# Compressing the decode requests' pages inside the first query tiles of the prompt attention

## The reference

```python
def cmp_sub(kv, w_cmp):
    B, T = kv.shape[:2]
    kb = kv.reshape(B, T // D_CMP, D_CMP, 2, KV_HEADS, N_HEAD_DIM)
    first = jnp.einsum('bnpchd,cpde->bnche', kb, w_cmp[:, :D_CMP])
    second = jnp.einsum('bnpchd,cpde->bnche', kb, w_cmp[:, D_CMP:])
    return first, second

def compress_blocks(first, second, w_cmp, pe_cmp):
    bias = jnp.einsum('cpd,cpde->ce', pe_cmp, w_cmp)
    return first[:, :-1] + second[:, 1:] + bias[None, None, :, None, :]
```

## Time and profile before

| | |
|---|---|
| Median of 3 runs | 1217.35 us (1217.02 to 1221.65) |
| Profiled execution, its own time | 1223.5 us |
| Its span | 1221.7 us, 14579 instructions |
| PE busy | 1127.9 us (92%) |
| DVE / ACT / POOL busy | 478.2 / 325.7 / 71.8 us |
| Mean granted clock of TensorE | 0.953 of full |
| Chain that ended last | PE 84%, DVE 9%, ACT 3%, issue 2%, DMA 1% |

### The profile page before, as it was taken

How to read it: one execution, slowest core, us unless ns; L and a number is a source line. 1 busy time by engine, 2 the same in 40 slices (tenths; PEclk the granted TensorE clock), 3 DMA queues, 4 the chain that set the end, 5 groups by cost and what they waited for, 6 DMA issues and landing times.

```text
span 1221.7 us, 14579 instructions
## 1 busy us (share of the span) xinstructions
PE 1127.9 (92%) x5447; PEld 664.1 (54%) x5447; DVE 478.2 (39%) x1025; ACT 325.7 (27%) x791; POOL 71.8 (6%) x181
## 2 busy tenths in 40 slices
PE   5999999999999999999789999999967869679997
PEld 4566644444455656966554566665555628244442
DVE  6453430001112221323377776776545443421121
ACT  4421100000011111100256666676641102001110
POOL 1000000000000001110111000010050002000000
PEclk9999999999999999999789999999977869879999
DMA  9202010203100303110210000000042543722221
GB/s 321 120 1 69 1 69 0 71 3 68 44 28 1 80 13 88 41 57 1 83 57 1 1 2 1 1 2 1 1 135 86 139 130 116 236 69 69 69 69 43
DMA packets 70222, 73.00 MB, mean 60 GB/s; under 512 B 28411, under 2 KB 54695, under 8 KB 70087
## 3 DMA queue, kind: packets, MB, share of 16 engines
q1 hardware_dynamic: 70150, 72.06, 19.4%
HBM read 62.14 MB, written 14.07 MB: 62 GB/s over the span
## 4 chain that ended last, share of the span: by engine, by line
PE 84%; DVE 9%; ACT 3%; issue 2%; DMA 1%; SPq 0%; POOL 0%; ACTq 0%; DVEq 0%; POOLq 0%
PE PS L1893 25%; PE PS L1886 12%; PE PS L2235 10%; PE PS L2001 7%; PE PS L2020 5%; PE PS L2033 5%; PE PS L1937 3%; PE PS L2173 2%; PE PS L2169 1%; PE PS L1923 1%; DVE VV L1665 1%; PE PS L2007 1%; PE PS L2126 1%; ACT XT L1113 1%; PE PS L1891 1%
## 5 line engine op out<-in xcount | busy, mean ns | idle before, releaser
L1893 PE MATMUL PS<-WR,XT 128*128 128x512 f32 (+1 forms) x768 | 306.9, 557 | 0.0
L1893 PEld LDWEIGHTS PS<-WR,XT 128*128 128x128 f32 x768 | 144.0, 190 | 147.7 <-issue 144.6
L1886 PE MATMUL PS<-XT,WR 128*128 128x352 f32 x576 | 172.2, 460 | 1.1 <-ACT QN L998 1.1
L1886 PEld LDWEIGHTS PS<-XT,WR 128*128 128x128 f32 x576 | 108.8, 190 | 61.2 <-ACT QN L998 1.6
L1493 DVE TENSOR_REDUCE XT<-PS 128x1 f32<-128x640 f32 (+7 forms) x128 | 84.5, 701 | 37.7 <-PE PS L2007 37.7
L2001 PE MATMUL PS<-KTR,XT 64*128 64x512 f32 (+3 forms) x384 | 92.8, 502 | 5.8 <-ACT XT L1113 5.4
L1113 ACT ACTIVATE XT<-PS,XT 128x640 f32<-128x640 f32 (+7 forms) x96 | 66.7, 701 | 10.4 <-DVE XT L1493 10.4
L2001 PEld LDWEIGHTS PS<-KTR,XT 64*128 64x128 f32 x384 | 45.7, 192 | 36.9 <-issue 16.8
L2020 PE MATMUL PS<-cst,XT 128*128 128x128 f32 x396 | 61.9, 281 | 0.8 <-ACT MT L1126 0.8
L2235 PE MATMUL PS<-WR,QT 128*128 128x512 f32 x128 | 57.6, 593 | 0.6 <-DVE XT L1733 0.6
L2235 PE MATMUL PS<-WR,KT 128*128 128x512 f32 x128 | 57.5, 592 | 0.0
(11 more groups left out here) (445 smaller groups left out, 1358.7 us busy)
## 6 DMA issues: line engine op xcount, KB each, us to landing
WR<-in_w_in SPq DMA_DIRECT2D x24, 512.0 KB, 6.3
WR<-in_cache_kv_cmp SPq DMA_DIRECT2D x48, 128.0 KB, 2.5
WR<-in_w_in SPq DMA_DIRECT2D x32, 128.0 KB, 3.1
KVN<-in_cache_kv_sel SPq DMA_DIRECT2D x32, 128.0 KB, 2.1
GM<-in_cache_kv_sel SPq DMA_DIRECT2D x32, 128.0 KB, 2.0
QN<-in_cache_kv_win SPq DMA_DIRECT2D x8, 512.0 KB, 5.6
XT<-in_x_prompt SPq DMA_DIRECT2D x8, 512.0 KB, 4.1
out_y_prompt<-XT SPq DMA_DIRECT2D x8, 512.0 KB, 2.9
```

The lines of the kernel that those rows point to most:

```text
L1886: ins = mm(b[:, 0:THIRD], w[:, k, r // 3 * P:(r // 3 + 1) * P], xt[:, k, r % 3 * THIRD:(r % 3 + 1) * THIRD], **f)
L1893: ins = mm(b[:, 0:width], xt[:, k, r * P:(r + 1) * P], w[:, k, :], **f)
```

## The change

The eight requests are compressed in pairs 0 to 25 of the prompt attention. In pair p < 24 TensorE turns chunk p mod 3 of request p // 3, in every third pair the fourth chunk as well; from pair 2 on one half of the products, the other half, and the turn of the values follow in rotation. Products use PSUM bank 3, chunks bank 1, which short tiles leave free. ScalarE's copies and VectorE's sums take the matching places in their lists, GpSimd sorts in tiles 0 to 3. SyncE loads all eight requests' compressed pages in a row (three buffers instead of four), then the output weights and the first half's window rows, all during the attention. The results lie in `kc_all` and `vc_all` until the decode step reads them. The turned weights are stored in another order of dimensions. The decode step has no compression left.

```diff
...
+        def chunk_of(p):
+            return (p // 3, p % 3) if p < 3 * SB else None
+        def event_of(p):
+            return (("cmp", (p - 2) // 3, (p - 2) % 3) if (p - 2) % 3 < 2 else ("turn", (p - 2) // 3, 0)) \
+                if 2 <= p < 2 + 3 * SB else None
...
-            for b in range(4):
+            for b in range(SB):
                 load_cmp(b)
...
+            sp.wait_ge(cm_sorted, SB + 1)
+            for c in range(KC):
...
+            sp.wait_ge(qr_turned, NT)
+            load_windows(0)
...
             sp.wait_ge(num_done, MH)
             load_pages(0, 0)
-            for g in range(2):
-                sp.wait_ge(cmp_done, 2 * (4 * g + 4 + 1))
-                load_windows(g)
-                if g == 0:
-                    for b in range(4, SB):
-                        load_cmp(b)
-                    sp.wait_ge(g_pe, GPE(0, "sel"))
-                    load_pages(1, 1)
-                    load_pages(1, 0)
...
-            sp.wait_ge(cm_sorted, SB + 1)
-            for c in range(KC):
...
+            sp.wait_ge(g_pe, GPE(0, "sel"))
+            load_pages(1, 1)
+            load_pages(1, 0)
+            sp.wait_ge(g_pe, GPE(0, "win"))
+            load_windows(1)
...
+            def sort_sample(b):
+                pool.wait_ge(cm_s_in[b % 3], (b // 3 + 1) * NPG * 16)
+                if b >= 2:
+                    pool.wait_ge(cx_turned, 4 * (b - 1) + 4)
+                for a in range(4):
+                    ins = nc.gpsimd.tensor_copy(sorted_s[b % 2][a].rearrange("p (c r d) -> p c r d", c=4, r=2),
+                                                cms[b % 3][:, a, :].rearrange("p (r c d) -> p c r d", c=4, r=2))
+                ins.then_inc(cm_sorted, 1)
             pool.wait_ge(proj_done, ALL)
+            nc.gpsimd.memset(kc_all, 0.0).then_inc(blocks_zeroed, 1)
...
                 rotate(x, trig[:, i, :], NH, rq).then_inc(q_rot, 1)
+                if i in (2, 3):
+                    sort_sample(4 if i == 2 else 7)
...
                 nc.gpsimd.tensor_tensor(p8, p8, sum8.unsqueeze(2).broadcast_to([P, NH, NCMP]), ALU.mult).then_inc(pc_scaled, 1)
...
-            pool.wait_ge(qr_turned, NT)
-            sort_sample(0)
+                if i == 0:
+                    pool.wait_ge(vc_ready, 1)
+                for b in ((0, 1), (2, 3), (5, 6))[i] if i < 3 else ():
+                    sort_sample(b)
...
-            sort_sample(1)
-            pool.wait_ge(cm_sorted, 3)
...
+            def take_pairs(b, ch):
+                act.wait_ge(cx_turned, 4 * (b + 1) + ch + 1)
+                if b and ch % 2 == 0:
+                    act.wait_ge(cmp_done, 2 * b + ch // 2 + 1)
+                nc.scalar.activation(cx_s[:, ch // 2, ch % 2, :, :], bank(1).rearrange("p (n s) -> p s n", s=8), ACT.Copy)\
+                    .then_inc(cx_ready, 1)
...
                 if p + 1 < NT * PAIRS:
                     for h in range(KVH):
                         exps(p + 1, h)
+                chunk = chunk_of(p)
+                if chunk:
+                    take_pairs(*chunk)
                 take_turned(p, 1)
+                if chunk and chunk[1] == 2:
+                    take_pairs(chunk[0], 3)
...
-            compress_act(1, cxs)
...
+                event = event_of(p)
+                if event:
+                    what, b, c = event
+                    if what == "cmp":
+                        sum_blocks(b + 1, c, vct_bd if c else kc_all[:, b, :])
+                    else:
+                        take_values(b + 1, vc_all[:, b, :])
...
+            def turn_pairs(b, ch):
+                pe.wait_ge(cm_sorted, b + 2)
+                pe.wait_ge(cx_ready, 4 * (b + 1) + ch)
+                for a in range(4):
+                    ins = nc.tensor.transpose(bank(1)[:, a * P:(a + 1) * P], sorted_s[b % 2][a][:, ch * P:(ch + 1) * P], ident)
+                ins.then_inc(cx_turned, 1)
...
                 if p + 1 < NT * PAIRS:
                     scores(p + 1)
                 turn_weights(p, 0)
+                event, chunk = event_of(p), chunk_of(p)
+                if event:
+                    what, b, c = event
+                    if what == "cmp":
+                        products(b + 1, c, cx_s)
+                    else:
+                        turn_values(b + 1)
...
                 if p >= 2:
                     values(p // 2 - 1, p % 2)
+                if chunk:
+                    turn_pairs(*chunk)
                 turn_weights(p, 1)
+                if chunk and chunk[1] == 2:
+                    turn_pairs(chunk[0], 3)
...
-            turn_values(1)
-            products(2, cxs)
...
-            turn_values(2)
...
-            pe.wait_ge(vc_ready, 3)
...
-                for j in range(4):
-                    q = 1 + 4 * g + j
-                    if q > 2:
-                        turn_pairs(q, sorted_slot(q - 1))
-                        if j and q > 3:
-                            turn_values(q - 1)
-                        products(q, cxs)
-                turn_values(q)
...
```

More of the change, by code:

```diff
@@ L275, in build @@
         qraw = from_xt(2 * GQ * P).rearrange("p (s x) -> p s x", s=2)
-        pairs3 = from_xt(2048)
+        kc_all, vc_all = (from_xt(SB * P).rearrange("p (b x) -> p b x", b=SB) for _ in range(2))
         wc = WR[:, 6144:8192].rearrange("p (c s f e) -> p c s f e", c=2, s=8, f=2)
@@ L360, in build @@
         wpages = QN[:, 0:4096].rearrange("p (j n c) -> p j n c", j=4, n=WIN // P)
[L362 to L367, removed]
+        cms = [WR[:, n * 2048:(n + 1) * 2048].rearrange("p (a x) -> p a x", a=4) for n in range(3)]
+        sorted_s = [[VV[:, 2048 + a * 512:2560 + a * 512] for a in range(4)],
+                    [pp_a[:, 0, 512:1024], pp_a[:, 1, 512:1024], pp_a[:, 2, 512:1024], MT[:, 4608:5120]]]
         ktb = VV[:, 0:2048].rearrange("p (s x) -> p s x", s=2)
@@ L494, in build @@
         num_done = sem("num_done")
-        cm_s_in = [sem(f"cm_s_in{n}") for n in range(4)]
+        cm_s_in = [sem(f"cm_s_in{n}") for n in range(3)]
         page_in = [sem(f"page_in{n}") for n in range(2)]
@@ L918, in _ @@
             nc.gpsimd.memset(rtmp, 0.0).then_inc(f_zero, 1)
-            for b in range(2, SB):
-                if b == 4:
-                    pool.wait_ge(ktb_used, 8)
-                if b == 5:
-                    pool.wait_ge(g_pe, GPE(0, "win"))
-                sort_sample(b)
         ZEROS = 8
@@ L1193, in _ @@
             for g in range(2):
-                for j in range(4):
-                    if j == 0 and g:
-                        act.wait_ge(g_pe, GPE(0, "win"))
-                    if 4 * g + j >= 2:
-                        compress_act(1 + 4 * g + j, cxs)
                 for src, what, c in ((scs[:, 0:P], "cmp_max", c_cmp), (ps_[0], "max0", c_br[0]), (ps_[1], "max1", c_br[1])):
@@ L2194, in _ @@
                 for j in range(4):
-                    mm(bank(6)[rows_j(j), 0:P], scs[:, P + 32 * j:P + 32 * j + 32], vc_g[:, j, :], start=True, stop=False,
+                    mm(bank(6)[rows_j(j), 0:P], scs[:, P + 32 * j:P + 32 * j + 32], vc_all[:, 4 * g + j, :], start=True, stop=False,
                        skip_group_check=True)
```

147 lines of the change are left out of this document (62 added, 85 removed).

## The result

The changed kernel takes **1260.5 us** (median of 4 runs, 1254.7 to 1262.8); the kernel before, run beside it, 1219.1 (1217.0 to 1221.7). The ratio is 1.031, with a 95% interval of 1.026 to 1.036: slower by 3%, or 41 us. The forecast was 1248, with a range of 1232 to 1264.

A forecast was written before the change was run, and what follows sets the result against it. TensorE was taken to bound the attention stage, compression and page loads side by side the decode step. Attention +36 and decode -4.6 gave +31.4 us on 1217.35, so 1248 us, range 1232 to 1264 (the forecast's own 1236 to 1260).

The forecast's parts named there:

- the pairs get longer than their work: Rival, attention pairs: ScalarE's in-order queue holds back exponentials, 12 us more in all, 1260 to 1268; chance 0.09.
- Bound of the attention stage: Prompt attention tiles: TensorE bounds them, so added work is paid for except in gaps; +36 us for eight requests.
- both stay under the length that a pair then has: Attention pairs: VectorE (busy 22 of 31 us in tile 2) and ScalarE (20 of 31) take their added work within a pair.
- a wait for the third chunk's copy: Attention pairs: TensorE waits for ScalarE's copy before turning a request's fourth chunk; 0.3 x 8, within tiles 1 and 2.
- To the first load: Decode step until the states are done: waits behind the compression go, first half's page loads move 5.2 us earlier.
- Loads to the first keys from GM: Decode step, first half: keys turned 7.6 us earlier, only 2.4 us come through, the rest a wait of some 10 us.
- Sums to keys: Decode step, second half: 38.1 us from the sums to the keys instead of 40.1; 2.0 us won.
- The sharpest mark: Decode step, second half: sums-to-keys distance at 38 us; the forecast is wrong if it is under 30.
- The clock: Decode step: half clock after each of two new page waits costs 2.5 us, 5 for both.
- the page loads take the compression's place: Decode step: page loads are nearly as late as the compression before them, so removing it wins little; decode in all -4.6 us.
- page loads do not hold the decode step: Rival, decode step: pages land in time, gains are 43.5 us, the kernel gets faster at 1210; chance 0.05.
- The output weights: Before the projection: earlier loads bring nothing, and in the attention stage they meet empty queues.

The follow-up runs named there:

- e1: Changed kernel with VectorE's block sums and takes put before the shift and sum of the compressed branch; 1247.2 us, ratio 1.022 to the kernel before.
- e4: Kernel of e1 with TensorE turning a pair's chunk before it multiplies with the values; 1236.7 us, ratio 1.016 to the kernel before.
- e2: Fixed addresses in the 64 loads of the selected pages: in the changed kernel 1234.9 us, in the kernel before 1223.8 us (ratio 1.003).
- e7: Changed kernel with the output weights' loads put back behind the second half's windows, as in the kernel before; 1256.6 us, ratio 1.028 to the kernel before.
- e9: Changed kernel with the edits of e1, e4 and e5 together; 1214.1 us, ratio 0.996 to the kernel before.
- e5: Kernel of e1 with the selected pages' loads shared between SyncE and GpSimd, each reading its own page numbers; 1222.8 us, ratio 1.003 to the kernel before.
- e6: Kernel of e1 with SyncE reading 16 page numbers into registers before its waits; 1233.7 us, ratio 1.013 to the kernel before.

## Why the forecast was right, and where its terms were not

**The number.** By the two profiles the change is +39.3 us, against +31.4 forecast: 14.9 more in the attention stage and 7.0 less in the decode step. That the sum came within 12 us of the measured time is partly luck, since the two errors have opposite signs. The time also lies just outside the 1236 to 1260 that I gave the forecast itself and at the lower edge of the rival "the pairs get longer than their work" (1260 to 1268, chance 0.09); the mechanism is that rival's as much as the forecast's. And the range was not quite what its working says: the ends +17 and +52 on 1217 are 1234 and 1269, not 1232 and 1264.

**Bound of the attention stage: right.** Work put into the tiles was paid. The sum of +36 is what e1 measures (+36.3) with the same work in another order. By tiles it was 11.6, 11.0, 13.2 and 0.5, read at the same instruction of each (forecast 7, 13, 14.5, 1.5): tile 0 hides less than I gave it, tile 1 more. So the agreement of the sum is partly luck too: e1 still holds 4.4 us of waits for the third chunks' copies, for which I had named 2.4 and put only about 1 into the tiles.

**The step that failed** is the sentence "both stay under the length that a pair then has", said of VectorE and ScalarE. It compares busy time with the length of a pair, and the busy time was right. What counts is where in the list the new instruction stands and what stands in front of it. I had written of a wait for the third chunk's copy (0.3 x 8 forecast, 4.4 measured, of which e4 leaves 0.7) and had not looked at the pairs in which VectorE's list has a wait for another engine ahead of the block sums. Those are pairs 1 and 2 of each tile (`SHIFT`, `SUM`). The rival "the pairs get longer than their work" named the right kind of cause and the wrong engine and place: in one pair of a tile ScalarE's list holds back one exponential, L1093, and VectorE's list hands that on (5.4 of the 8.9 us); in another VectorE's list waits for TensorE's compressed scores (3.5).

**Decode step, -4.6 forecast, -11.6 measured**, term by term:
- To the first load: -5.2 forecast, -5.6 measured. Right.
- Loads to the first keys from GM: -2.4 forecast, -3.6. SyncE took 17.3 us for the 16 loads where I had kept the 18.3 of the earlier trace rows. The wait before them is 5.1 us, not 10. TensorE stood 3.2 us for the gates (L1645), which the compression had covered, and a product of the keys from KVN ran at half clock; both lie in the shadow of the loads and cost nothing:

```profile
999.77 0.66 PE L2172 MATMUL PS<-XT 128*32 128x128 f32 x8 [3.19 <-DVE KTR L1645]
...
1003.31 3.62 PE L2165 MATMUL PS<-VV,XT 128*32 128x512 f32 x4
```

- Sums to keys: -2.0 forecast, -2.5 measured (37.6 us where I had said 38.1). The sharpest mark held. Most of the wait stands before the keys from KVN, 16.2 of 22.6 us, where I had named only GM's.
- **The clock, +5.0 forecast, 0.0 measured.** It is the mis-sized term. The half clock behind each wait was there. One window behind the second wait for GM (columns as above):

```profile
1092.00:1095.00 3.00, 3.00 (x7) 1.06 (x7) 1.83 (x8) 0.00 (x0) 0.00 (x0) 0.50 1.09 357
```

The Trainium skill's rule (TensorE: Matmul & The Clock Gate, "HAM oscillation — how this bites in real kernels"), that each wait for data lets the next piece start cold, agrees with such rows. The stretch at 1044 of the kernel before, which I took for a case of it, is none: no wait for a DMA stands in front of it, only waits for VectorE of 1.6 us and less. The kernel before had half clock in the same phases, later in them, so only the difference counts. From the keys to the sums' end it was 35.4 us after and 37.1 before (-1.8); from the second keys to the projection 40.5 and 38.8 (+1.8).

These sums hide two parts. Directly behind the waits, from the keys from GM to L2182 (L2192 before), it is 9.95 us instead of 9.04 in the first half and 10.77 instead of 9.02 in the second: 2.7 us together, which is the price of the two waits and half of my 5.0. The rest of the first half's phase is 25.4 us instead of 28.1 and gives it back, in a phase that varies by itself (last section); that of the second is the same (29.8 and 29.7). I had priced the fall that I added too high and left out those that were there already; that the net is 0.0 and not 2.7 is chance as far as the rows show.

**That the page loads take the compression's place: right**, and shown by e2 from both sides. The rival "page loads do not hold the decode step" is refuted by the same runs: its mark, under 30 us from the sums to the keys, is 37.6.

**The output weights: right** so far as e7 can tell.

## What to carry to other kernels

Before work is moved off a chain, look for the second chain that runs beside it; here 47 us of compression stood in front of page loads that were as late, so moving it could win some 16 us, and it cost 51 where it went. In a stage bound by one engine, the place of each added instruction in the other engines' lists matters more than their busy share: an instruction that is ready must not stand behind one that waits. And if loads with addresses from a table are late, count the sequencer's time for each load first: a second queue, or numbers read ahead of the wait, halved it.

## What the runs showed of the hardware

The same phase, with the same instructions, takes 32 to 38 us from one profile to another. It is the one after the keys from GM, where products of 2 us alternate with short waits for VectorE. The row of the changed kernel, then that of e9:

```profile
1016.86:1052.97 36.11, 26.01 (x173) 12.60 (x173) 15.86 (x37) 2.11 (x4) 0.00 (x0) 0.69 0.00 1
```

```profile
991.86:1024.41 32.55, 21.49 (x174) 10.94 (x173) 15.84 (x37) 2.11 (x4) 0.00 (x0) 0.90 0.00 1
```

173 and 174 instructions, and 26.0 against 21.5 us of them, at a mean granted clock of 0.69 and 0.90. VectorE's busy time is the same to 0.02 us. The longest wait of TensorE inside is 3.0 us in either. The last phase goes the same way (34.5 to 40.4 us). Over the eleven profiles of kernels with the changed decode step the two phases together take 67.3 to 76.5 us, and what sets the level is open. Each profile is of another kernel, so they can't tell how much goes with the edit and how much with the execution. Executions of one kernel do differ: e9's twelve took 1212.4 to 1226.5 us, at a mean granted clock of 0.964 down to 0.944. But the two kernels with the chunk early are 10.5 (e4 against e1) and 8.8 us (e9 against e5) faster by the medians and only 3.8 and 4.7 in the attention stage, so a part that goes with the edit isn't excluded. It is worth up to 9 us in one execution, more than several of the effects that were looked for, and it is why the differences above are read from marks and not from medians alone.

An issue of a load with a fixed address (e2), or one already in a register (e6), costs SyncE 0.5 us; with its read of the table 1.1 (17.3 us for 16 in the changed kernel). GpSimd needs 1.15 for the latter (e5).
